# Stick-breaking attention over pairs of heads: masks and suffix sums accumulated by TensorE into the banks of the scores

## What is computed

```
z = einsum('bqhd,bkhd->bhqk', q, k) * scale + bias
mask = k_pos[None, :] < q_pos[:, None]
log_keep = where(mask, log_sigmoid(-z), 0.0)
after = cumsum(log_keep, axis=3, reverse=True) - log_keep
att = where(mask, exp(log_sigmoid(z) + after), 0.0)
out = einsum('bhqk,bkhd->bqhd', att, v)
```

## Time and profile before

| | us |
|---|---|
| three runs: median (lowest to highest) | 3156.99 (3144.64 to 3160.9) |
| profiled execution: its own time | 3163.61 |
| profiled execution: span | 3161.9 |
| PE busy (matmul) | 3008.1 |
| DVE busy | 1407.7 |
| ACT busy | 939.9 |
| POOL busy | 346.0 |

### The profile page before, as it was taken

The page is one execution under the profiler, slowest core; times in us unless marked ns, Lnnn a source line. Parts: engine busy times, 40 slices in busy tenths (PEclk is TensorE's granted clock), DMA queues, the critical chain, the costliest instruction groups (busy, mean ns, idle before and its releaser), DMA issues.

```text
span 3161.9 us, 51816 instructions
## 1 busy us (share of the span) xinstructions
PE 3008.1 (95%) x20978; PEld 2804.8 (89%) x20978; DVE 1407.7 (45%) x1805; ACT 939.9 (30%) x1389; POOL 346.0 (11%) x464
## 2 busy tenths in 40 slices
PE   7999999988997799999989999999899999999997
PEld 7999999968887499999989999999665669999997
DVE  4434357635542554343553443335333335434355
ACT  3222234342220232222341422223344433222233
POOL 3000012103320210000110000001122211000011
PEclk9999999988995699999999999999778779999998
DMA  4232222210002222322222422222111102222321
GB/s 122 67 89 83 80 80 81 92 39 2 2 2 55 67 80 80 89 84 80 67 80 83 133 91 80 80 82 87 58 54 53 53 27 85 88 80 80 89 70 56
DMA packets 306819, 225.35 MB, mean 71 GB/s; under 512 B 8014, under 2 KB 300287, under 8 KB 306687
## 3 DMA queue, kind: packets, MB, share of 16 engines
q1 hardware_dynamic: 306674, 224.30, 23.3%
q0 software_dynamic: 64, 0.00, 0.0%
HBM read 212.14 MB, written 12.13 MB: 71 GB/s over the span
## 4 chain that ended last, share of the span: by engine, by line
PE 91%; DVE 4%; issue 2%; ACT 2%; POOL 1%; DMA 1%; another core or an unknown queue 0%; DVEq 0%; SPq 0%; POOLq 0%; ACTq 0%
PE ps L445 70%; PE ps L1503 2%; PE ps L1528 2%; PE ps L1517 2%; PE ps L1002 2%; PE ps L1531 1%; PE ps L1015 1%; PE ps L1012 1%; PE ps L1470 1%; PE ps L1489 1%; PE ps L1082 1%; PE ps L1094 1%; PE ps L1057 1%; PE ps L1461 1%; DVE w_lo L421 0%
## 5 line engine op out<-in xcount | busy, mean ns | idle before, releaser
L445 PE MATMUL ps<-hx_hi,w_hi 128*128 128x320 f32 (+1 forms) x3986 | 852.1, 295 | 12.2 <-DVE hx_lo L1567 7.7
L445 PE MATMUL ps<-hx_hi,w_lo 128*128 128x320 f32 (+1 forms) x3986 | 850.4, 294 | 0.0
L445 PE MATMUL ps<-hx_lo,w_hi 128*128 128x320 f32 (+1 forms) x3986 | 849.7, 294 | 0.0
L411 ACT ACTIVATE w_hi<-raw 128x1024 fp32r<-128x1024 f32 (+2 forms) x378 | 381.5, 1011 | 1302.1 <-PE ps L445 1285.3
L445 PEld LDWEIGHTS ps<-hx_hi,w_hi 128*128 128x128 f32 x3986 | 611.6, 189 | 14.9 <-issue 7.0
L445 PEld LDWEIGHTS ps<-hx_hi,w_lo 128*128 128x128 f32 x3986 | 610.6, 188 | 0.0
L445 PEld LDWEIGHTS ps<-hx_lo,w_hi 128*128 128x128 f32 x3986 | 608.9, 188 | 0.0
L421 DVE TENSOR_TENSOR w_lo<-raw,w_hi 128x1024 fp32r<-128x1024 f32 (+2 forms) x378 | 470.2, 1244 | 120.3 <-ACT w_hi L411 120.0
L445 PE MATMUL ps<-hid_hi,w_hi 128*128 128x320 f32 (+1 forms) x1664 | 356.9, 295 | 11.6 <-DVE of L907 8.3
L445 PE MATMUL ps<-hid_hi,w_lo 128*128 128x320 f32 (+1 forms) x1664 | 355.7, 295 | 0.0
L445 PE MATMUL ps<-hid_lo,w_hi 128*128 128x320 f32 (+1 forms) x1664 | 355.6, 295 | 0.0
(11 more groups left out here) (367 smaller groups left out, 2825.2 us busy)
## 6 DMA issues: line engine op xcount, KB each, us to landing
raw<-in_ffn_w_in SPq DMA_DIRECT2D x176, 512.0 KB, 4.9
raw<-in_ffn_w_out SPq DMA_DIRECT2D x64, 512.0 KB, 4.3
raw<-in_a_w_in SPq DMA_DIRECT2D x33, 512.0 KB, 4.4
raw<-in_ffn_w_out SPq DMA_DIRECT2D x32, 384.0 KB, 3.4
raw<-in_ple_w_gate SPq DMA_DIRECT2D x16, 512.0 KB, 4.0
raw<-in_w_kv SPq DMA_DIRECT2D x16, 512.0 KB, 4.0
k_page<-in_cache_k SPq DMA_DIRECT2D x16, 512.0 KB, 4.0
v_page<-in_cache_v SPq DMA_DIRECT2D x16, 512.0 KB, 4.3
```

The costliest lines, as they stand in the source:

```text
L411: nc.scalar.activation(w_hi[:, m, 0:k], s.view(m, slot), ACT.Copy).then_inc(w_hi_done, 1)
L445: last = nc.tensor.matmul(TILE[m][:, c0:c1], w[:, m, k], h[:, k, c0:c1], start=k == 0 and a == 0, stop=k == k_all - 1 and a == 2)
```

## The change

- The scores of a pair of heads lie in five whole banks, and all steps go by pair. Bank A of a head holds key block 0 (512 queries), bank B block 1 (384) and block 3 (128), bank C block 2 of both heads (256 each). Bank 5 takes the outputs of both heads, 6 the key transposes, 7 the pages.
- `hide` adds -1e30 to the diagonal blocks by one fp32r matmul of an identity with a `future` tile per bank. POOL's masks go.
- `sums` multiplies softplus by `minus_ones` and `minus_tril` and accumulates into the bank that holds the scores. DVE's subtraction goes; ACT takes Exp with the bias straight from PSUM (`weights`).
- DVE's cap and maximum read the scores in PSUM and add the bias; ACT's copy of z goes. Exp and Ln run over whole banks of 512.
- The loop is written out for all eight pairs, so matmuls address kT, qT and v_tok directly, and POOL's copies go.
- B and C are called near, A far. Matmuls of the two heads stand next to each other. Semaphore `c_first` stands between the two heads' scores in bank C.
- The scores of the first pair come ahead of the new tokens' part, which moves into the first pair and to banks 6 and 7.
- The order of the pages' steps in a pair is: sums and the first two transposes among the pair's sums; page outputs of the sequence before behind the near scores; page scores at the end.

```diff
         r = Region(hx0, hx1)
         q_blocks = r.take("q_blocks", [P, NP, 2, NB, TD])
-        k_heads = r.take("k_heads", [P, 2, TP])
-        q_heads = r.take("q_heads", [P, 2, TP])
-        v_heads = r.take("v_heads", [P, 2, PT, P])
-        zb = r.take("zb", [P, 2, WALL])
-        ls = r.take("ls", [P, 2, WALL])
+        ls = r.take("ls", [P, 2, ZW])
+        att = r.take("att", [P, ZW])
+        minus_tril = r.take("minus_tril", [P, P])
+        minus_ones = r.take("minus_ones", [P, P])
...
+        scores = ps[:, 0:5].rearrange("p b n -> p (b n)")
+        O_BANK, K_BANK, PAGE_BANK = 5, 6, 7
+        BANK_A, BANK_B, BANK_C = (0, 1024), (512, 1536), 2048
+        QC = TP // 2
+
+        def keys(t, a, b):
+
+            first = (BANK_A[a], BANK_B[a], BANK_C + a * QC, BANK_B[a] + TP - P)[b]
+            return t[:, first:first + TP - b * P]
...
-
-            def copies(pair, par):
-
-                nc.gpsimd.tensor_copy(k_heads[:, par:par + 1], kT[:, ds(pair, 1), 0:TP]).then_inc(at["copied"], 1)
-                nc.gpsimd.tensor_copy(q_heads[:, par:par + 1], qT[:, ds(pair, 1), 0:TP]).then_inc(at["copied"], 1)
-                nc.gpsimd.tensor_copy(v_heads[:, par], v_tok[:, 0:PT, ds(pair * P, P)]).then_inc(at["copied"], 1)
-                nc.gpsimd.tensor_copy(bias_c[:, par], bias_b[:, ds(pair * 2, 2)]).then_inc(at["copied"], 1)
-
-            def masks(u, c, j):
-
-                a = c % 2
-                d = slice(AT[j], AT[j] + P)
-                pool.wait_ge(at["max"], u + 1)
-                nc.gpsimd.tensor_tensor(ls[:, a, d], ls[:, a, d], lt[:], ALU.mult).then_inc(at["keep"], 1)
-                nc.gpsimd.tensor_tensor(zb[:, a, d], zb[:, a, d], neg_lt[:], ALU.add).then_inc(at["mask"], 1)
-
-            pool.wait_ge(at["q_sample"], 2)
...
+            def weights(n, g, first, a, width):
+                act.wait_ge(at["r"], 5 * n + g)
+                return nc.scalar.activation(att[:, first:first + width], scores[:, first:first + width], ACT.Exp, bias=bias_of(n, a))
+
...
+            for n in range(NP):
+                weights(n, 1, BANK_C, 0, QC)
+                weights(n, 1, BANK_C + QC, 1, QC).then_inc(at["att"], 1)
+                for a in range(2):
+                    weights(n, 2 + a, BANK_B[a], a, 512).then_inc(at["att"], 1)
+                if n:
+                    page_weights(n - 1)
...
+                for a in range(2):
+                    weights(n, 4 + a, BANK_A[a], a, 512).then_inc(at["att"], 1)
...
+                if n + 1 < NP:
+                    exps(n + 1, BANK_B + (BANK_C,), 0)
+                    lns(n + 1, BANK_B + (BANK_C,), 0)
...
+                    exps(n + 1, BANK_A, 3)
+                act.wait_ge(at["o_head"], n + 1)
+                nc.scalar.activation(hid_hi[:, n, 0:TP], ps[:, O_BANK], ACT.Copy).then_inc(hid_hi_done, 1)
+                if n + 1 < NP:
+                    lns(n + 1, BANK_A, 3)
...
+            def capped(n, g, first, a, width):
+
+                dve.wait_ge(at["z"], 5 * n + g)
+                return nc.vector.tensor_scalar(ls[:, n % 2, first:first + width], scores[:, first:first + width],
+                                               bias_of(n, a), SOFTPLUS_CAP, ALU.add, ALU.min)
+
+            def softplus(n, g, first, a, width):
+
+                dve.wait_ge(at["l"], 5 * n + g)
+                part = ls[:, n % 2, first:first + width]
+                return nc.vector.scalar_tensor_tensor(part, scores[:, first:first + width], bias_of(n, a), part, ALU.add, ALU.max)
+
+            def near(step, n, counted):
+
+                for a in range(2):
+                    step(n, 1 + a, BANK_B[a], a, 512).then_inc(counted, 1)
+                step(n, 3, BANK_C, 0, QC)
+                step(n, 3, BANK_C + QC, 1, QC).then_inc(counted, 1)
+
...
+            def score(n, a, b, first):
+
                 rows_ = slice(a * HD, (a + 1) * HD)
+                return mm(keys(scores, a, b), kT[rows_, n, b * P:(b + 1) * P], qT[rows_, n, b * P:TP],
+                          start=first, stop=False, skip_group_check=True)
+
+            def hide(first, every):
+
+                part = bank_of(scores, first).rearrange("p (x n) -> p x n", n=P)[:, 0:4:every]
+                x = 4 // every + (every == 3)
+                mm(part, ident_r[:], future[:].unsqueeze(1).to_broadcast((P, x, P)), start=False, stop=False,
+                   skip_group_check=True).then_inc(at["z"], 1)
+
+            def near_scores(n):
+                if n:
+                    pe.wait_ge(at["att"], 5 * n - 2)
+                for b in (1, 3):
+                    for a in range(2):
+                        score(n, a, b, b == 1)
+                score(n, 0, 2, True).then_inc(at["c_first"], 1)
+                hide(BANK_B[0], 3)
+                hide(BANK_B[1], 3)
+                pe.wait_ge(at["c_first"], n + 1)
+                score(n, 1, 2, False)
+                hide(BANK_C, 2)
+
+            def far_scores(n):
+                if n:
+                    pe.wait_ge(at["att"], 5 * n)
+                for a in range(2):
+                    score(n, a, 0, True)
+                for a in range(2):
+                    hide(BANK_A[a], 4)
+
+            def sums(n, a, b):
+                for b2 in range(PT - 1, b, -1):
+                    mm(keys(scores, a, b)[:, (b2 - b) * P:], minus_ones[:], keys(ls[:, n % 2], a, b2), start=False, stop=False,
+                       skip_group_check=True)
+                return mm(keys(scores, a, b), minus_tril[:], keys(ls[:, n % 2], a, b), start=False, stop=True,
+                          skip_group_check=True)
+
+            def weigh(n, b):
+                for a in range(2):
+                    last = mm(ps[a * HD:(a + 1) * HD, O_BANK, b * P:], v_tok[:, b, n * P + a * HD:n * P + (a + 1) * HD],
+                              keys(att, a, b), start=b == PT - 1, stop=b == 0, skip_group_check=True)
+                return last
...
+            for m in range(2):
+                pe.wait_ge(evac[m], s.n["unit"] if m == 0 else s.n["eb"])
+            near_scores(0)
+            far_scores(0)
             new_scores()
-            scores((0, 0, 0), 0, 0)
-            scores((1, 0, 1), 0, 1)
-            new_sums()
-            scores((2, 0, 2), 0, 2)
-            scores((3, 0, 3), 0, 3)
-            new_outputs()
-            pe.wait_ge(at["new_out"], 2)
-            turns(pe, turn_)
+            pe.wait_ge(at["minus"], 2)
+            for n in range(NP):
+                pe.wait_ge(at["max"], 5 * n + 3)
+                sums(n, 0, 2)
+                sums(n, 1, 2).then_inc(at["r"], 1)
+                for a in range(2):
+                    sums(n, a, 3)
+                    sums(n, a, 1).then_inc(at["r"], 1)
+                if n:
+                    page_sums(n - 1)
+                    k_transposes(n, 0)
+                else:
+                    new_sums()
+                for a in range(2):
+                    pe.wait_ge(at["max"], 5 * n + 4 + a)
+                    sums(n, a, 0).then_inc(at["r"], 1)
+                if n == 0:
+                    new_outputs()
+                    pe.wait_ge(at["new_out"], 2)
+                    k_transposes(n, 0)
+                k_transposes(n, 1)
+                if n + 1 < NP:
+                    near_scores(n + 1)
+                if n:
+                    page_outputs(n - 1)
+                k_transposes(n, 2)
+                pe.wait_ge(hid_done, s.n["hid"] + n)
+                pe.wait_ge(at["att"], 5 * n + 3)
+                for b in (3, 2, 1):
+                    weigh(n, b)
+                k_transposes(n, 3)
+                if n + 1 < NP:
+                    far_scores(n + 1)
+                pe.wait_ge(at["att"], 5 * n + 5)
+                weigh(n, 0).then_inc(at["o_head"], 1)
+                page_scores(n)
+            page_sums(NP - 1)
+            page_outputs(NP - 1)
             pe.wait_ge(at["o_lo_page"], 2 * NB)
             pe.wait_ge(hid_done, s.n["hid"] + KD)
```

More of the change, by code:

```diff
@@ L1290, in turn_ @@
-            def turn_(turn, last):
-                for n in range(NU):
-                    logs(unit_of(turn, n + 2, last))
-                    if n and n % PT == 0:
-                        output(turn, n // PT - 1)
-                    u, c, j = unit_of(turn, n, last)
-                    part = zb[:, c % 2, AT[j]:AT[j] + W[j]]
-                    act.wait_ge(at["sub"], u + 1)
-                    nc.scalar.activation(part, part, ACT.Exp).then_inc(at["att"], 1)
-                    scores(unit_of(turn, n + 3, last))
-                    page_step(turn, n)
-                output(turn, PT - 1)
@@ new lines, in page_outputs @@
+            def page_outputs(n):
+                pe.wait_ge(v_page_in, 32 * (n + 1))
+                pe.wait_ge(at["att_page"], n + 1)
+                for pg in range(NPG):
+                    for f in range(NP):
+                        c = slice(f * 2 * TD, (f + 1) * 2 * TD)
```

(3 more changed lines are left out.)

410 lines of the change are left out of this document (164 added, 246 removed).

## The result

| | before | after |
|---|---|---|
| median of the runs, us | 3156.55 (3144.64 to 3160.9, 4 runs) | 3116.25 (3112.3 to 3119.03, 4 runs) |
| profiled execution: span | 3161.9 | 3117.2 |
| ahead of the stage / stage / behind it | 2233.0 / 356.7 / 572.2 | 2260.6 / 271.8 / 584.8 |

The ratio is 0.9877, with a 95% interval of 0.9848 to 0.9907. 3116 us lies inside the forecast's range, but the gain is 40 us where 72 were forecast. The last line of the table says how that came about: the attention stage lost 85 us, more than forecast, and the rest of the program, in which the diff changes only a few of POOL's instructions that make constants at the start, gained 40.

A forecast was written before the change was run, and what follows sets the result against it. PE was taken as the bound, its time being columns, changes of shape and clock. Stage 12 + 285 - 24 + 7 + 5 = 285 us for 356.7, 72 less, gave 3085 us (median 3157 before), range 3060 to 3122.

The forecast's parts named there:

- What bounds it: Attention loop: PE is the bound, busy 325.5 of 328.9 us; relieving DVE, ACT and POOL buys nothing by itself.
- covers of the softplus: PE work hiding softplus in each pair: 14 us for near softplus's 8, 9 us for far softplus's 5.
- rival 3: Attention loop: PE waits for the softplus, 3 us per pair, 24 us; 3109 us, or 3133 without overlap; chance 0.12.
- Work on PE: Per pair: five hide matmuls add 0.6 us, changes of shape fall from 26 to 12; 29.7 us for 31.5, high clock.
- The clock: Attention loop: low stretches of 5 us behind page scores and 6.8 behind page outputs per pair; another 28 us saved.
- Rivals 2 and 4: Attention loop: clock high throughout, 3062 us, with overlap 3042, chance 0.08; low from page outputs into near sums, 3192, chance 0.05.
- Two halves at once: Neighbouring score and weigh matmuls of two heads overlap, saving each meeting's shorter record: 2.45 us per pair, 24 us.
- rival 1: Score and weigh matmuls on the array's two halves do not overlap: 3109 us; chance 0.30.
- Head and tail: Attention stage's ends: head 12 us for 25.8, net gain 7 with new tokens' 7 us; tail 5 for 2.0, loss 3.
- 12 + 7 + 5: Attention stage outside the eight pairs: head 12 us, new tokens moved into pair 0 with waits 7, tail waits 5.
- Stage 12 + 285 - 24 + 7 + 5 = 285 us for 356.7: Attention stage: head 12, eight pairs 285, overlap minus 24, new tokens 7, tail 5; 72 us less.

The follow-up runs named there:

- split blocks: Changed kernel with an unused 32-byte spacer, its blocks of 32 sixteen-column page matmuls cut in two, one page each: 3056.69 us, ratio to before 0.9679.
- 32 bytes less: eps moved into gain's unused end, so scratch0 and all behind it lie 32 bytes lower: changed kernel 3119.25 us; kernel before 3188.34 us for 3154.03.
- everything shifted: Changed kernel with 32 bytes less, with the region of all tiles, weights too, begun 32 bytes later: 3121.06 us.
- the block: Changed kernel with an unused 32-byte tile put where bias_c stood, so hx_hi and all behind it lie as before: 3079.93 us, ratio to before 0.976.

## Why the prediction was right and wrong

**The stage: 271.8 us for 285 forecast.**
- *What bounds it.* Right: PE is 91% of the chain, its waits in the loop are 4.2 us, none for `ls`. The covers of the softplus held, and rival 3 fell.
- *Work on PE.* Right. A pair would take 25.8 us at the high clock; the forecast had 29.7 - 2.45 = 27.25, and the difference is the overlap's (below). The five `hide` took 0.43 + 0.32 + 0.37 = 1.1 us with three changes of shape at 0.17, so 0.6 without, as forecast.
- *The clock.* Right: 6.8 us low from the page outputs on and 3.4 behind the page scores, 10.2 for 11.8 forecast; the loop's mean clock is 0.83, as forecast. Worth 0.8 us per pair, some 6 us in eight. Rivals 2 and 4 fell. The split blocks bear out the cause that the forecast read from the earlier trace rows, the sixteen-column matmuls: with the same matmuls and no waits, blocks of sixteen brought the clock of seven pairs from 0.84 to 0.91. They did not end the falls, five of which came behind the second half of the page outputs, so what sets the moment of a fall stays open. The Trainium skill's account ("TensorE: Matmul & The Clock Gate", section on the oscillation of the clock) puts a fall down to gaps of waiting, and here it fell at 2416.7, some two microseconds into the block of page outputs, with PE busy for all 6.80 us of the window ahead of it. Falls behind waits are in this trace too, at the start of the loop: at 2276.8, 2290.5 and 2300.7 PE had been idle for 1.8 to 2.2 us shortly before. These go with waits, as the page has it; the one at 2416.7 does not.
- *Two halves at once.* Right in kind, and rival 1 fell; the size was too small. The forecast saved the shorter record of a meeting, as if the second pass of one ran beside the first pass of the next. Both passes run beside both: four records of 512 take 1.06 us for 1.88, four of `weigh` 1.01 for 1.88, the near scores 1.49 for 2.13 + 0.17, the near `weigh` 1.45 for 2.56 + 0.17. That is 3.78 us per pair for 2.45 forecast, 1.3 us more, 11 to 13 us in eight pairs.
- *Head and tail.* Eight pairs of 30.94 are 247.5 us; the other 24.3 are what the forecast gave to head, new tokens and tail (12 + 7 + 5). Inside it, the first sums started at 2269.4, 9 us behind the last product for 12, and the tail's page outputs ran wholly at the low clock, 6.99 us.

So the stage saved 85 us, and the 13 us beyond the forecast are the overlap and a little of the clock. One trace of each kernel doesn't fix that sum to better than some 13 us, though: the instructions of before with 32 bytes less had a stage of 343.6 us for 356.7, by the clock alone (below), while the changed kernel's was 271.8 us as it stands, 269.5 with 32 bytes less, 269.4 with everything shifted and 272.2 with the block.

**Everything else: 40 us lost, forecast nothing.** The step that failed is the sum itself: "Stage 12 + 285 - 24 + 7 + 5 = 285 us for 356.7: 72 us less. The profiled execution took 3163.6 us and would take 3092". It takes the rest of the program over unchanged. The diff has the reason in one line, the removed `bias_c`, and neither the forecast nor a rival looked at where the tiles behind it then lie. The kernel before shows little of it: six windows of 40 us have 306 to 308 products, and nearly all products have the same distance but for multiples of 2048 bytes (the tiles from `hx_hi` to `hid_lo` begin 18432 bytes apart, `w_lo` begins 8192 behind `w_hi`). The exception was there to be seen, the few products from `p_hi` and `p_lo`, at 149 ns for 146. With the 32 bytes back the changed kernel takes 3080 us, 5 below the forecast of 3085. That the range held 3116 is luck: rival 1 and part of rival 3 had stretched it upwards, and the mechanism was not in it.

## What to carry to other kernels

When a change adds or drops a tile, print every tile's address before and after, and if an operand of the busiest loop has moved against the weights, put the bytes back or try two or three other distances; the sign is the count of matmuls in windows in which PE is always busy at the full clock, several windows and not one. Matmuls on the two 64-wide halves of the array belong together with nothing 128-wide between them, and then cost little more than one of them. Where sixteen-column matmuls come in a long block, cut the block and put wide matmuls between; blocks of sixteen for thirty-two gave 16 us of 272 here, a finer cut nothing that is settled.

## What the hardware showed that was not expected

- A shift of 32 bytes between moving operand and weights changed an fp32r matmul of 320 columns from 145.6 to 148.7 ns and one of 256 columns from 116.9 to 118.0, and a program of some 3100 us by 34 to 36 us, with no instruction changed. Other distances gave 143.8 to 148.4 ns; no rule was found.
- An f32 matmul of two records on one half of the array overlaps fully with its neighbour on the other half: 1.45 us for both heads' near `weigh`, 1.44 for one head's alone.
- PE started matmuls of the other half past three records that stand before them in the program.
- The same instructions with other addresses had a stage of 343.6 us at a clock of 0.77 and one of 356.7 us at 0.76 in the loop and 0.54 ahead of it: the product of length and clock is 265 us for both. The product tells work from clock: it is 223 us for the stage of the changed kernel with the block and with the pages' blocks halved, though the second is 16 us shorter.
